# A group of x turned on VectorE and moved by 16 transfers, and ordered first transfers, in a fused three-block kernel

## The reference

```python
# layer 0: pool and conformer mixer, then MLP; layer 1: short-conv mixer, then MLP
h = rms_norm(x, mix_pre_g[layer]); m = mixer(h)          # one matmul in, one out
x = x + rms_norm(m, mix_post_g[layer])
h = rms_norm(x, ffn_pre_g[layer])
x = x + rms_norm(relu(h @ w1) ** 2 @ w2, ffn_post_g[layer])
# last layer: attention and spatial gating from one projection of rms_norm(x), then w_out
```

## Time and profile before

| what | value |
|---|---|
| median of 3 runs | 2687.98 us (2687.74 to 2688.13) |
| profiled execution | 2690.7 us, its span 2689.0 us |
| PE busy | 2679.8 us, 12001 matmuls and transposes |
| DVE, ACT, POOL busy | 1872.4, 1292.8, 278.2 us |
| transfers | 515.58 MB, mean 192 GB/s |

### The profile page before, as it was taken

The page is one execution under the profiler, slowest core; times in us unless marked ns, Lnnn a source line. Parts: engine busy times, 40 slices in busy tenths (PEclk is TensorE's granted clock), DMA queues, the critical chain, the costliest instruction groups (busy, mean ns, idle before and its releaser), DMA issues.

```text
span 2689.0 us, 31099 instructions
## 1 busy us (share of the span) xinstructions
PE 2679.8 (100%) x12001; PEld 2218.5 (83%) x12001; DVE 1872.4 (70%) x2495; ACT 1292.8 (48%) x1635; POOL 278.2 (10%) x263
## 2 busy tenths in 40 slices
PE   9999999999999999999999999999999999999999
PEld 7888888888888888888888888888888888888887
DVE  6878777666866767776677676667767757765564
ACT  6765544434444454444544444344445446544452
POOL 4851100000000010000110000000011001000000
PEclk9999999999999999999999999999999999999999
DMA  7545665555555556555555555555555645455554
GB/s 248 183 169 180 215 211 183 184 202 188 193 192 195 194 183 213 193 197 194 187 188 204 203 188 186 190 188 203 188 188 179 211 173 182 169 200 194 188 188 156
DMA packets 267972, 515.58 MB, mean 192 GB/s; under 512 B 8450, under 2 KB 27956, under 8 KB 267316
## 3 DMA queue, kind: packets, MB, share of 16 engines
q1 hardware_dynamic: 267556, 513.34, 55.4%
q10 hardware_dynamic: 272, 0.26, 0.0%
HBM read 511.47 MB, written 2.10 MB: 191 GB/s over the span
## 4 chain that ended last, share of the span: by engine, by line
PE 98%; DMA 1%; DVE 1%; ACT 0%; issue 0%; SPq 0%
PE bank L786 32%; PE bank L788 32%; PE bank L787 32%; PE bank L837 1%; DMA x_res<-in_x 0%; DMA w_raw<-in_ab_w_in 0%; PE bank L854 0%; PE bank L1027 0%; DVE w_lo L765 0%; PE bank L988 0%; PE bank L1041 0%; PE bank L1014 0%; DVE w_lo L755 0%; DVE bank L1783 0%; PE bank L1048 0%
## 5 line engine op out<-in xcount | busy, mean ns | idle before, releaser
L765 DVE TENSOR_TENSOR w_lo<-w_raw,w_hi 128x1024 fp32r<-128x1024 f32 x952 | 1183.1, 1265 | 493.5 <-ACT w_hi L747 487.8
L747 ACT ACTIVATE w_hi<-w_raw 128x1024 fp32r<-128x1024 f32 x956 | 974.7, 1056 | 589.9 <-PE bank L788 432.9
L786 PE MATMUL bank<-w_hi,A_lo 128*128 128x512 f32 x2432 | 952.5, 392 | 2.3 <-DVE A_lo L1468 0.8
L788 PE MATMUL bank<-w_hi,A_hi 128*128 128x512 f32 x2432 | 947.2, 389 | 0.0
L787 PE MATMUL bank<-w_lo,A_hi 128*128 128x512 f32 x2432 | 946.7, 389 | 0.0
L786 PE MATMUL bank<-w_hi,B_lo 128*128 128x512 f32 x1408 | 548.7, 390 | 0.0
L788 PE MATMUL bank<-w_hi,B_hi 128*128 128x512 f32 x1408 | 547.9, 389 | 0.0
L787 PE MATMUL bank<-w_lo,B_hi 128*128 128x512 f32 x1408 | 547.8, 389 | 0.0
L786 PEld LDWEIGHTS bank<-w_hi,A_lo 128*128 128x128 f32 x2432 | 456.6, 188 | 98.4 <-DVE w_lo L765 2.3
L788 PEld LDWEIGHTS bank<-w_hi,A_hi 128*128 128x128 f32 x2432 | 456.4, 188 | 95.8
L787 PEld LDWEIGHTS bank<-w_lo,A_hi 128*128 128x128 f32 x2432 | 456.7, 188 | 93.2
(11 more groups left out here) (178 smaller groups left out, 975.7 us busy)
## 6 DMA issues: line engine op xcount, KB each, us to landing
w_raw<-in_ffn_w SPq DMA_DIRECT2D x256, 1024.0 KB, 5.1
w_raw<-in_w_in SPq DMA_DIRECT2D x88, 1024.0 KB, 4.9
w_raw<-in_sc_w_in SPq DMA_DIRECT2D x48, 1024.0 KB, 5.1
w_raw<-in_ab_w_out SPq DMA_DIRECT2D x16, 1024.0 KB, 5.0
w_raw<-in_sc_w_out SPq DMA_DIRECT2D x16, 1024.0 KB, 5.1
w_raw<-in_w_out SPq DMA_DIRECT2D x16, 1024.0 KB, 5.3
w_raw<-in_ab_w_in SPq DMA_DIRECT2D x28, 512.0 KB, 4.6
w_raw<-in_ab_w_in SPq DMA_DIRECT2D x8, 1024.0 KB, 5.1
```

What stands on the lines that cost most here:

```text
L747: e.activation(w_hi[:, s % SPLIT_SLOTS, :], raw_step(s), ACT.Copy).then_inc(hi_made, 1)
L765: e.tensor_tensor(w_lo[:, slot, :], raw_step(s), w_hi[:, slot, :].bitcast(F32), ALU.subtract).then_inc(lo_made, 1)
L786: e.matmul(ps, lo[:, kt, tok], wh, start=first, stop=False)
L788: ins = e.matmul(ps, hi[:, kt, tok], wh, start=False, stop=last)
```

## The change

Group 3 of x is no longer turned by PE in stages 1 to 4. After the last update DVE makes four transposes (`turn_last`), each of 128 partitions by 256 elements, in which every 32x32 block is turned within its own 32 partitions, from x to `x_quads` (the memory of `conv_in`). Then SP issues 16 transfers of 32 partitions by 1 KB (`move_x`), which bring each block row to its partitions in `x_T` (the memory of `conv_out`). ACT and DVE cast from there (`hi_moved`, `lo_moved`) at f+8, ahead of the statistics, instead of at f+6. At the start, SP waits before most of its first transfers until an earlier one has landed, load 2 goes by rows as loads 0 and 1 do, six steps instead of four are split in halves, and the casts of group 1 alternate with splits. DVE's last taps move one step ahead. Two waits of later stages name other semaphores, as the old ones no longer stand for the buffers.

```diff
@@ small_banks @@
+        if key[0] == "pre" and key[1] > 0 and key[2:3] == (NG - 1,):
+            continue
@@ build @@
+        x_quads = conv_in_flat[:, 0:GK * TOK]
+        x_T = conv_out_flat[:, GK * TOK:2 * GK * TOK]
...
-        BEGIN = 2 * STEPS_PER_LOAD
+        BEGIN = RAW_SLOTS * STEPS_PER_LOAD
@@ sync_program @@
+            def move_x(p):
+                e.wait_ge(x_turned.sem, x_turned.of(p))
+                for q in range(4):
+                    for r in range(4):
+                        e.dma_start(x_T[32 * r:32 * r + 32, q * TOK:(q + 1) * TOK],
+                                    x_quads[32 * q:32 * q + 32, r * TOK:(r + 1) * TOK]).then_inc(x_moved, 16)
...
             e.dma_start(x[:, :, CH // 2:CH], x_dram[:, :, CH // 2:CH]).then_inc(x_loaded[0], 16)
+            e.wait_ge(x_begun, 16)
             load_rows(0, 2)
+            e.wait_ge(rows_loaded[0], 16)
             load_rows(0, 3)
+            e.wait_ge(rows_loaded[1], 16)
             load_x(1)
-            for k in range(GK):
-                load_rows(1, k)
+            e.wait_ge(x_loaded[0], 16)
+            load_rows(1, 0)
+            e.wait_ge(rows_loaded[2], 16)
+            load_rows(1, 1)
+            e.wait_ge(rows_loaded[3], 16)
+            load_rows(1, 2)
+            load_rows(1, 3)
+            e.wait_ge(x_loaded[1], 16)
             load_x(2)
-            load_weights(2)
+            e.wait_ge(rows_loaded[4], 16)
+            load_rows(2, 0)
+            e.wait_ge(rows_loaded[5], 16)
+            load_rows(2, 1)
+            e.wait_ge(rows_loaded[6], 16)
+            load_rows(2, 2)
+            load_rows(2, 3)
+            e.wait_ge(x_loaded[2], 16)
             load_x(3)
...
                 load_weights(n)
+                for p in range(1, 5):
+                    if n == S0[STAGE[p]] // STEPS_PER_LOAD + 5:
+                        move_x(p)
@@ pe_program, and alike in stage 4 and pe_mlp @@
-                if c == C_L1 + 1 and i in (0, 2):
-                    turn_x(2, 2 + i // 2)
+                if (c, i) == (C_L1 + 1, 0):
+                    turn_x(2, 2)
@@ act_program @@
+            def hi_moved(p):
+                e.wait_ge(x_moved, 256 * p)
+                for k in range(GK):
+                    kt = GK * (NG - 1) + k
+                    ins = e.activation(by_32(halves["A"][0][:, kt, :]), moved(k), ACT.Copy, scale=par_col(PRE_COL[p], kt))
...
-                if (c, i) == (STAGE[p] + 1, 2):
-                    hi_x(p, 3)
                 if (c, i) == (STAGE[p], 4):
+                    hi_moved(p)
                     statistics(p)
...
-            hi_x(0, 1)
+            for h in two:
+                hi_half(0, 1, h)
+                split_to(e, split_hi, at, STEPS_PER_LOAD + h)
@@ dve_program (early and the first group as in act_program) @@
+            def turn_last(p):
+                e.wait_ge(x_made.sem, x_made.of(p - 1, NG - 1, 1))
+                blocks = x[:, :, (NG - 1) * CH:].rearrange("p t (k c) -> p t k c", k=GK)
+                for r in range(4):
+                    out = x_quads[:, r * TOK:(r + 1) * TOK].rearrange("p (t k c) -> p t k c", t=NT, k=GK)
+                    ins = e.transpose(out, blocks[:, :, :, 32 * r:32 * r + 32])
+                ins.then_inc(x_turned(p), 1)
+
+            def lo_moved(p):
+                hi, lo = halves["A"]
+                for k in range(GK):
+                    kt = GK * (NG - 1) + k
+                    e.wait_ge(hi_cast.sem, hi_cast.of("pre", p, NG - 1, k // 2))
+                    for tt in tiles:
+                        ins = e.scalar_tensor_tensor(by_32(lo[:, kt, :])[:, tt, :, :], moved(k)[:, tt, :, :],
+                                                     par_col(PRE_COL[p], kt), by_32(hi[:, kt, :].bitcast(F32))[:, tt, :, :],
+                                                     ALU.mult, ALU.subtract)
...
                     for tt in tiles:
                         update(p - 1, g, tt)
+                turn_last(p)
...
-                for tap in taps_at(DVE_TAPS, POS[c, i], DVE_TAP_TO):
-                    dve_tap(e, *tap)
+                s = POS[c, i]
+                for step in (s, s + 1) if s == DVE_TAP_TO - 2 else (s,) if s < DVE_TAP_TO - 1 else ():
+                    for tap in taps_at(DVE_TAPS, step, DVE_TAP_TO):
+                        dve_tap(e, *tap)
@@ pool_program, ahead of the third stage @@
-            e.wait_ge(lo_cast.sem, lo_cast.of("silu", 1, 1))
+            e.wait_ge(x_moved, 256 * 2)
```

More of the change, by code:

```diff
@@ L371, in build @@
         x_loaded = [semaphore(f"x_loaded{i}") for i in range(NG)]
-        x_begun = semaphore("x_begun")
-        BEGIN = 2 * STEPS_PER_LOAD
-        rows_loaded = [semaphore(f"rows_loaded{i}") for i in range(2 * GK)]
+        x_begun, x_moved = semaphore("x_begun"), semaphore("x_moved")
+        BEGIN = RAW_SLOTS * STEPS_PER_LOAD
+        rows_loaded = [semaphore(f"rows_loaded{i}") for i in range(RAW_SLOTS * GK)]
         half_hi = semaphore("half_hi")
@@ L448, in build @@
                                    ([(g, tt) for tt in tiles for g in gs] if 0 in gs else [(g, tt) for g in gs for tt in tiles])])
+        x_turned = signal("x_turned", [(p,) for p in range(1, 5)])
         tap_done = signal("tap_done", DVE_TAPS)
@@ L604, in build @@
         for n in range(LOADS):
-            before = LOADED[n - RAW_SLOTS] if n >= RAW_SLOTS + 2 else 0
+            before = LOADED[n - RAW_SLOTS] if n >= 2 * RAW_SLOTS else 0
             LOADED.append(before + 16 * (2 if load_row[n][0] < 4 else 1))
@@ L966, in pe_program @@
                 r = c - C_L2
-                if r == 1 and i in (0, 2):
-                    turn_x(4, 2 + i // 2)
+                if (r, i) == (1, 0):
+                    turn_x(4, 2)
                 if since(c, i, C_L2) == 3:
@@ L1033, in pe_mlp @@
             for c, i in matmul_steps(e, p):
-                if c == up_chunk(layer, 0, 1) and i in (0, 2):
-                    turn_x(p, 2 + i // 2)
+                if (c, i) == (up_chunk(layer, 0, 1), 0):
+                    turn_x(p, 2)
         def pe_attention(e, aux_begin, task, h):
@@ L1084, in hi_scaled, with hi_half @@
                 e.activation(halves[buf][0][:, kt + 1, :], view[:, 1, :], ACT.Copy, scale=gains[1]).then_inc(hi_cast(*key), 1)
+            def hi_half(p, g, h):
+                kt = GK * g + 2 * h
+                hi_scaled("A", kt, [par_col(PRE_COL[p], kt + k) for k in two], "pre", p, g, h)
             def hi_x(p, g):
                 for h in two:
-                    kt = GK * g + 2 * h
-                    hi_scaled("A", kt, [par_col(PRE_COL[p], kt + k) for k in two], "pre", p, g, h)
+                    hi_half(p, g, h)
+            def hi_moved(p):
[3 more added lines that the diff above has]
+                    ins = e.activation(by_32(halves["A"][0][:, kt, :]), moved(k), ACT.Copy, scale=par_col(PRE_COL[p], kt))
+                    if k % 2 == 1:
+                        ins.then_inc(hi_cast("pre", p, NG - 1, k // 2), 1)
             def hi_tile(p, g, tt):
@@ L1266, in act_program @@
                         act_sigmoids(e, r, lambda tt: att[:, tt, j * CH:(j + 1) * CH],
-                                     (lo_cast.sem, lo_cast.of("h", 1, NB - 1, 1, 1)))
+                                     (lo_cast.sem, lo_cast.of("pre", 4, NG - 1, 1)))
                     elif r < 10:
@@ L1339, in act_program, with by_32, moved @@
                                          ACT.Copy).then_inc(hi_cast("merged", g, h), 1)
+        def by_32(v):
+            return v.rearrange("p (t q c) -> p t q c", t=NT, q=4)
+        def moved(k):
+            return x_T.rearrange("p (q t k c) -> p t k q c", q=4, t=NT, k=GK)[:, :, k, :, :]
         def layer_of(c):
@@ L1470, in lo_scaled, with lo_half @@
                 ins.then_inc(lo_cast(*key), 1)
+            def lo_half(p, g, h):
+                kt = GK * g + 2 * h
+                lo_scaled("A", kt, [par_col(PRE_COL[p], kt + k) for k in two], "pre", p, g, h)
             def lo_x(p, g):
                 for h in two:
-                    kt = GK * g + 2 * h
-                    lo_scaled("A", kt, [par_col(PRE_COL[p], kt + k) for k in two], "pre", p, g, h)
+                    lo_half(p, g, h)
+            def turn_last(p):
[14 more added lines that the diff above has]
+                                                     ALU.mult, ALU.subtract)
+                    if k % 2 == 1:
+                        ins.then_inc(lo_cast("pre", p, NG - 1, k // 2), 1)
             def lo_part(p, g, tt, h):
@@ L1578, in early @@
                     lo_x(p, 2)
-                if (c, i) == (STAGE[p] + 1, 2):
-                    lo_x(p, 3)
                 if (c, i) == (STAGE[p], 4):
+                    lo_moved(p)
                     statistics(p)
@@ L1589, in dve_program @@
                 at[0] += 1
-            lo_x(0, 1)
+            for h in two:
+                lo_half(0, 1, h)
+                split_to(e, split_lo, at, STEPS_PER_LOAD + h)
```

## The result

| kernel | median | runs | ratio to before, 95% interval |
|---|---|---|---|
| before | 2687.99 us (2687.74 to 2688.13) | 6 | |
| after | 2697.99 us (2696.66 to 2698.54) | 6 | 1.0036 (1.0025 to 1.0047) |

The change makes the kernel 10.0 us slower. The prediction said 2682.5 us, with 2686.4 as the upper end. The profiled execution of after took 2696.66 us, with a span of 2694.9: 5.9 more than the span before. So 4.1 us of the 10.0 are not in the comparison of the two profiles, and have to be found too.

What follows compares the result with a forecast made beforehand. PE was taken to bound the kernel, busy 2679.8 of 2689.0 us. Turns 3.6, taps 0.5 and start 1.4 sum to 5.5 us gained, taking the median from 2688.0 to 2682.5 us; range 2680.2 to 2686.4.

Steps and rivals of the forecast that it cites:

- The turns: Stages 1 to 4: dropping PE's eight transposes of x's last group gains 0.89 us each time, 3.6 us in all.
- The chain at the boundary: Stage boundary: transposes, 16 issues, landing and casts finish before PE needs them at f+10, with 1.7 us of slack.
- both limits: Stage 1 boundary: PE's need of f+10 and of f+12 each allow the last move to land up to 279.8.
- rival 2: Boundaries: SP's issues are held in a backlog of their own, moves come late; 2715 us at 1 us an issue; chance 0.06.
- T: Stage 1 boundary: the time when all sixteen moves have landed, forecast as 278.1.
- rival 3: Boundaries: last move lands in 5.0 to 6.0 us, PE waits 1.6 to 5.6 us in all; 2686.1 us; chance 0.12.
- The loads behind the moves: Boundaries: SP's load of f+12 and f+13, queued behind the 16 moves, still comes in time; cost 0, cover 2 us.
- The taps: Layer norm: last tap and joins one step sooner release PE's 16 transposes earlier, gaining 0.5 us.
- The start: First transfers up to step 6: ordered landings shorten PE's waits, at most 3.9 us; 1.4 us gained was taken.
- The late end: Start: load 3's second half lands at 28.0, a loss of 0.5 us; as a rival 2684.4 us, chance 0.28.
- signs of being wrong: An idle PE ahead of f+10 or f+12, or load 3 landing after 27.5.
- the early end: Start: without a backlog group 2 lands near 14.3 and load 3's second half at 25.4, gaining 2.1 us.

Runs made afterwards that it cites:

- turns_free: no_start with neither PE's turn of group 3 nor the transposes and moves replacing it, so its output is not the reference's: 2684.46 us.
- taps_only: Kernel before with only DVE's last taps one step sooner: 2688.09 us.
- no_start: Changed kernel with the start of the kernel before, keeping the moved group 3 and the sooner taps: 2690.23 us.
- diag_moves: no_start with twelve moves instead of sixteen, all on SP; four small VectorE transposes write the other blocks: 2685.07 us.
- split_moves: no_start with five of the sixteen moves issued by ACT's queue instead of SP's: 2684.63 us.
- start_nowait: Kernel before with the new start but without SP's waits between the first transfers: 2687.77 us.
- the idle turns: Two runs: kernel before with the new start alone, plus 28 or 38 unread identity transposes on PE ahead of step 6: 2695.31 and 2692.99 us.

## Why the prediction was wrong, point by point

- **The turns, 3.6 us.** Right: 0.89 each from the trace, 0.90 measured by turns_free.
- **The chain at the boundary.** Its structure and both limits were right, one price was not. The step that failed is "16 x 0.39 = 6.2 us", taken from small loads out of DRAM: the moves go out 0.63 us apart from the first two on (272.75, 273.40), so it is not a backlog that builds up, which was rival 2's mechanism. The other terms: the four transposes 1.42 us for 1.7, the last landing 1.85 after its issue for 2.9. From the end of the last update (271.27) the last move lands 12.8 us later, not 10.8. In the clock of the kernel before that is T = 280.2, just where rival 3 begins (280.2 to 281.2; chance 0.12), though not by that rival's mechanism: the landing was quick, the issues were slow. The first half then follows at T + 2.25 (284.11 to 286.36), forecast T + 2.2.
- **The loads behind the moves.** "Cost 0, cover 2 us" failed for the same reason: issued 3.8 us later than forecast (12.25 us behind the last update, not 8.5), the load of f+12 is what stages 1 and 3 wait for. Rival 3 had 1.6 to 5.6 us for the waits in all; the runs give 5.2, so its number held by luck: the larger part of it in stages 1 and 3 is the wait for this load, which the rival did not have. Without the start the change would have been at 2690.2, outside the range as well.
- **The taps, 0.5 us.** Gained where forecast (0.54 at step 59), and 0.48 of it lost again five steps on. Nothing in the sum was for that.
- **The start, 1.4 us gained; measured 7.1 lost.** Three things failed. (1) "PE's waits there add up to 3.9 us": they were those of one execution, 2.7 us above the median, and the prediction carried those 2.7 us over as if they lay outside its argument, when they were most of what it meant to save. Other executions of the same start have 0.7 to 1.5 us of them (taps_only, no_start, turns_free, diag_moves). Only that of split_moves has 3.3, and it too was well above its median (1.8 us). (2) The late end was right as a time, and still set far too low as a loss. It had x's group 3 issued at 17.0 (16.70 in after), load 3 at 22.9 (22.44) and landed at 28.0 (28.98). But it was compared with the late 27.52 of that execution, where taps_only has load 3 landed at 24.82 and step 6 at 29.23: it is a loss of 4.1 us at step 6. (3) The sum left out the clock: 2.8 us in steps 6 and 7 (8.39 against 5.56). 4.1 + 2.8 = 6.9 us, close to the 7.1 of the medians. The prediction's own signs of being wrong all came: PE idle ahead of f+10 and f+12, and load 3 landing after 27.5.
- **Why not the early end.** Group 2 landed at 16.7, later than without the waits (14.4 in start_nowait, 15.1 in taps_only). The first packets are sooner (x's first 512 columns landed by 6.6, against 7.1 in taps_only), but each wait adds the time from an issue to its landing ahead of the next one. The steps up to 5 did get closer together (step 1 to step 5 took 13.0 us against 14.1 in taps_only), as forecast; that does not come from the waits, since start_nowait has it as well (13.05). It moves PE ahead into a longer wait for load 3.

## What to carry to other kernels

A queue that issues transfers has a length in time like an engine: before adding a wait or a small transfer to it, write down when the last big transfer behind it will go out, and against which step it has to land. Price an issue by one of the same kind, not by the nearest kind, and when its price decides a sign, look for a split over two queues or for fewer transfers first; here either made the whole cost vanish. Compare waits of a profiled execution with its distance from the median before counting them as a gain, and count a single long wait of PE dearer than its length.

## What the runs showed of the hardware that was not expected

- A move of 32 partitions by 1 KB from SBUF to SBUF takes its queue 0.63 us, about the same on ACT, where a load of 1 MB takes 0.37 to 0.43, the fourteen small loads 0.25 to 0.47 and the gain row 0.58. Why it is dearer is open. It lands 1.8 to 1.9 us after its issue starts (the first three at a boundary 2.3 to 2.5), with the next two already under way: the sixteen overlap and land some 0.6 us apart. The Trainium skill (DMA: Bandwidth & Descriptors, Anatomy of one DMA) gives about 2.0 us of fixed cost to a DMA that GpSimd issues. Here SP and ACT issue, and these landings take about as long, but not one behind another. The prediction read the figure as one for every DMA; nothing in its sum used it.
- ACT issues its moves while its own casts run: the five went out between 270.80 and 274.17 in split_moves, beside two splits. The casts of group 3 behind them began at 276.38, right at the last landing (276.35).
- An idle PE of 3.7 to 3.9 us was followed by 12 to 14 matmuls at the lower of the two levels of the clock, those of 2.4 and 2.0 us behind the idle turns by 8 to 9, those of 1.66 us (start_nowait), 1.07 us (split_moves) and less ahead of step 6 by none. The 1.8 us ahead of x's group 1 in after (from 10.5 to 12.3) and the waits of up to 1.3 us at its boundaries were followed by none either. What else sets it is open.
- Four VectorE transposes of 128x256 take 1.42 us together, 0.36 each: all 128 partitions in less than the 0.44 of one on 32 partitions.
- The same start varies by up to 3.0 us between the six profiled executions that have it (step 8 at 34.51 to 37.49). The two late ones are those in which x's group 1 and load 3 landed late (11.9 and 12.6, 27.0 and 27.5 us).
